# Third token mixer (HGRN2): at six of seven levels, scores only for one half of each block's queries, one bank per head, one copy out of it

## The reference, cut to what matters

```python
b = jnp.cumsum(gc, axis=2)
diff = b[:, :, :, None, :] - b[:, :, None, :, :]
pair_decay = jnp.where(causal[:, :, None], jnp.exp(jnp.minimum(diff, 0.0)), 0.0)
att = jnp.einsum('bhtd,bhsd,bhtsd->bhts', qc, kc, pair_decay)
o = jnp.einsum('bhtd,bhdv->bhtv', qc * jnp.exp(b), S) + jnp.einsum('bhts,bhsv->bhtv', att, vc)
```

## Time and profile before

| | |
|---|---|
| median of three runs | 2317.7 us |
| the profiled execution's own time | 2330.55 us |
| its span | 2328.8 us |
| TensorE matmul busy | 1913.3 us (82%) |
| TensorE weight load busy | 1544.2 us (66%) |
| VectorE busy | 1189.9 us (51%) |
| ScalarE busy | 662.1 us (28%) |
| mean granted TensorE clock | 0.864 of full speed |

### The profile page before, as it was taken

One profiled execution on the slowest core, in us unless ns is written; L12 is line 12 of the kernel. 1 busy time (PEld: TensorE's weight loads), 2 busy tenths in 40 slices (PEclk: granted clock), 3 DMA queues, 4 the chain that ended last, 5 costly groups with the idle time before them and its releaser, 6 DMA issues. The chain is left out here.

```text
span 2328.8 us, 28837 instructions
## 1 busy us (share of the span) xinstructions
PE 1913.3 (82%) x11780; PEld 1544.2 (66%) x11780; DVE 1189.9 (51%) x1853; ACT 662.1 (28%) x982; POOL 139.8 (6%) x160
## 2 busy tenths in 40 slices
PE   7997994787497986699999969899464989858996
PEld 5666773454396964588877756687343979648985
DVE  2473465652763523644442355446747745255655
ACT  3334324211220202422222253332412211034333
POOL 0000110000030300000000000000000303000000
PEclk9998996785698968799999979899686989678999
DMA  8201111670000003322222011122220000026441
GB/s 342 80 19 63 55 55 38 238 258 11 0 1 1 1 1 127 127 91 97 102 91 90 19 66 64 54 73 64 81 84 1 1 1 1 1 93 232 164 164 71
DMA packets 40884, 181.82 MB, mean 78 GB/s; under 512 B 4528, under 2 KB 5040, under 8 KB 32944
## 3 DMA queue, kind: packets, MB, share of 16 engines
q1 hardware_dynamic: 40752, 179.97, 21.8%
HBM read 178.91 MB, written 1.05 MB: 77 GB/s over the span
## 5 line engine op out<-in xcount | busy, mean ns | idle before, releaser
L211 PE MATMUL ps<-hr_in,wr_in 128*128 128x512 f32 (+1 forms) x544 | 224.8, 413 | 31.5 <-DVE wr_in L204 29.0
L211 PE MATMUL ps<-hr,wr 128*128 128x512 f32 (+1 forms) x704 | 240.4, 341 | 3.2 <-DVE wr L204 1.5
L212 PE MATMUL ps<-hr,wr 128*128 128x512 f32 (+1 forms) x704 | 237.5, 337 | 0.0
L213 PE MATMUL ps<-hr,wr 128*128 128x512 f32 (+1 forms) x704 | 237.3, 337 | 0.0
L212 PE MATMUL ps<-hr_in,wr_in 128*128 128x512 f32 (+1 forms) x544 | 211.9, 389 | 0.0
L213 PE MATMUL ps<-hr_in,wr_in 128*128 128x512 f32 (+1 forms) x544 | 211.5, 389 | 0.0
L204 DVE TENSOR_TENSOR wr<-pr,wr 128x2048 fp32r<-128x2048 f32 (+1 forms) x58 | 115.8, 1997 | 135.7 <-ACT wr L200 135.7
L211 PEld LDWEIGHTS ps<-hr_in,wr_in 128*128 128x128 f32 x544 | 109.7, 202 | 84.0 <-issue 33.7
L211 PEld LDWEIGHTS ps<-hr,wr 128*128 128x128 f32 x704 | 134.5, 191 | 21.9 <-DVE wr L204 6.7
L2108 ACT COPY pr<-ps 128x512 f32<-128x512 f32 x96 | 56.3, 587 | 324.1 <-PE ps L1747 324.1
L212 PEld LDWEIGHTS ps<-hr,wr 128*128 128x128 f32 x704 | 134.6, 191 | 13.7
(11 more groups left out here) (383 smaller groups left out, 3512.0 us busy)
## 6 DMA issues: line engine op xcount, KB each, us to landing
mix<-in_w_in SPq DMA_DIRECT2D x68, 512.0 KB, 3.6
pr<-in_w_up SPq DMA_DIRECT2D x28, 1024.0 KB, 4.9
ring<-in_ada_w SPq DMA_DIRECT2D x44, 512.0 KB, 4.6
mix<-in_w_up SPq DMA_DIRECT2D x16, 1024.0 KB, 5.0
hx<-in_ada_w SPq DMA_DIRECT2D x28, 512.0 KB, 6.4
pr<-in_w_down SPq DMA_DIRECT2D x14, 1024.0 KB, 4.9
pr<-in_ada_w SPq DMA_DIRECT2D x8, 1024.0 KB, 15.7
pr<-in_w_out SPq DMA_DIRECT2D x16, 512.0 KB, 7.1
```

What stands on the lines that cost most here:

```text
L211: nc.tensor.matmul(out, sh, mh, start=first, stop=False)
L212: nc.tensor.matmul(out, sh, ml, start=False, stop=False)
L213: return nc.tensor.matmul(out, sl, mh, start=False, stop=last)
```

## The change

For l = 0 nothing changes. For l > 0:

- `parts_of(n)` gives one part, with all tiles, in place of a part for each pair of tiles. `products(n)` counts the parts of the steps before n, and replaces `n * len(pairs)` in every wait.
- A matmul has as its moving operand only the half of each block's queries that counts, 64 columns in pieces of B/2 out of every B. The stationary operand stays as it was, the 128 keys. So the scores of one q for all tiles lie in one bank: eight times 64 columns in layer 0, four times 64 in layer 1. The number of matmuls is as before.
- `collect` copies each bank once, reading contiguous columns. In layer 0 this is two copies a step of 512 elements a partition, in place of four of 256. In layer 1 it is two of 256 as before.
- A step with l > 0 uses two banks and one raise of `s_mm`, so the six banks hold three steps in place of one and a half (layer 0).

```diff
-    pairs = tuple((j, j + 1) for j in js[::2])
+    whole = tuple((j, j + 1) for j in js[::2])
+    def parts_of(n):
+        return whole if steps[n][1] == 0 else (js,)
+    def products(n):
+        return sum(len(parts_of(k)) for k in range(n))
...
-            return ps[(2 * (n * len(pairs) + m) + q) % SCORES]
+            return ps[(2 * (products(n) + m) + q) % SCORES]
...
-                for m, jj in enumerate(pairs):
-                    used = 2 * (n * len(pairs) + m + 1)
+                for m, jj in enumerate(parts_of(n)):
+                    used = 2 * (products(n) + m + 1)
                     if used > SCORES:
                         pe.wait_ge(S("at"), used - SCORES)
-                    for b in range(4):
+                    for b in range(2 * len(jj)):
                         t0 = (b % 2) * T + jj[b // 2] * P
                         for q in range(2):
-                            mm = nc.tensor.matmul(score_bank(n, m, q)[:, b * P:(b + 1) * P], keys[d][q * HD:(q + 1) * HD, t0:t0 + P],
-                                                  queries[d][q * HD:(q + 1) * HD, t0:t0 + P], start=True, stop=True)
+                            key, query = (t[q * HD:(q + 1) * HD, t0:t0 + P] for t in (keys[d], queries[d]))
+                            out, n_out = score_bank(n, m, q), P
+                            if l:
+                                query, n_out = query.rearrange("p (b t) -> p b t", t=2 << l), HD
+                                query = query[:, :, 1 << l:] if d == 0 else query[:, :, :1 << l]
+                            mm = nc.tensor.matmul(out[:, b * n_out:(b + 1) * n_out], key, query, start=True, stop=True)
...
-                    o = d * 2048 + jj[0] * 512
+                    o, count = d * 2048 + jj[0] * 512, 2 * len(jj)
                     for q in range(2):
-                        dst = at[:, o:o + 1024].rearrange("p (b q t) -> p b q t", b=4, q=2)[:, :, q, :]
-                        src = score_bank(n, m, q)[:, :].rearrange("p (b t) -> p b t", b=4)
+                        dst = at[:, o:o + 256 * count].rearrange("p (b q t) -> p b q t", b=count, q=2)[:, :, q, :]
+                        src = score_bank(n, m, q)
...
-                            dst, src = (v.rearrange("p b (k t) -> p b k t", t=B)[:, :, :, part] for v in (dst, src))
+                            dst = dst.rearrange("p b (k t) -> p b k t", t=B)[:, :, :, part]
+                            src = src[:, 0:HD * count].rearrange("p (b k t) -> p b k t", b=count, t=B // 2)
```

More of the change, by code:

```diff
@@ L1399, in _ @@
                     job(p)
-            pe.wait_ge(S("at"), 2 * len(pairs) * len(steps))
+            pe.wait_ge(S("at"), 2 * products(len(steps)))
             for hd in range(HEADS):
@@ L1496, in factors @@
                 if n >= 2:
-                    dve.wait_ge(S("s_mm"), len(pairs) * (n - 1))
+                    dve.wait_ge(S("s_mm"), products(n - 1))
                 nc.vector.tensor_tensor(later(queries[d], d, l), later(expo[d], d, l), later(tiles(pr, T_HQ, 2), d, l), ALU.mult)
@@ L1504, in collect @@
                 B = 2 << l
-                for m, jj in enumerate(pairs):
-                    dve.wait_ge(S("s_mm"), len(pairs) * n + m + 1)
-                    o = d * 2048 + jj[0] * 512
+                for m, jj in enumerate(parts_of(n)):
+                    dve.wait_ge(S("s_mm"), products(n) + m + 1)
+                    o, count = d * 2048 + jj[0] * 512, 2 * len(jj)
                     for q in range(2):
-                        dst = at[:, o:o + 1024].rearrange("p (b q t) -> p b q t", b=4, q=2)[:, :, q, :]
-                        src = score_bank(n, m, q)[:, :].rearrange("p (b t) -> p b t", b=4)
+                        dst = at[:, o:o + 256 * count].rearrange("p (b q t) -> p b q t", b=count, q=2)[:, :, q, :]
+                        src = score_bank(n, m, q)
                         if l == 0:
-                            mask = c(C_BASE + d * P).bitcast(I32).rearrange("p (b t) -> p b t", b=1).to_broadcast([P, 4, P])
+                            src = src[:, :].rearrange("p (b t) -> p b t", b=count)
+                            mask = c(C_BASE + d * P).bitcast(I32).rearrange("p (b t) -> p b t", b=1).to_broadcast([P, count, P])
                         else:
                             part = slice(B // 2, B) if d == 0 else slice(0, B // 2)
-                            dst, src = (v.rearrange("p b (k t) -> p b k t", t=B)[:, :, :, part] for v in (dst, src))
+                            dst = dst.rearrange("p b (k t) -> p b k t", t=B)[:, :, :, part]
+                            src = src[:, 0:HD * count].rearrange("p (b k t) -> p b k t", b=count, t=B // 2)
                             mask = halves(c(C_LEVEL + (d * LEVELS + l) * P).bitcast(I32), B, d == 0).to_broadcast(list(dst.shape))
@@ L1603, in _ @@
                 if n >= 2:
-                    act.wait_ge(S("s_mm"), len(pairs) * (n - 1))
+                    act.wait_ge(S("s_mm"), products(n - 1))
                 nc.scalar.activation(sooner(keys[d], d, l), sooner(expo[d], d, l), ACT.Exp, scale=-1.0).then_inc(S("k_exp"), 1)
```

## The result

The changed kernel takes 2350.3 us (median of 4 runs, 2342.3 to 2355.8) beside 2319.2 us for the kernel before (4 runs, 2317.5 to 2323.4). The ratio is 1.013, 95% interval 1.009 to 1.016: slower by some 31 us. The forecast was slower by 5.8 us, 2323.5, range to 2333; the sign was right and the size was not.

The account below looks back on a forecast made before the run. Layer 0's score loop was taken as bound by TensorE and the loads its jobs pace. Terms: -1 (copies, tails, waits), +5.8 and +1 (clock in layers 0 and 1), +5.8 on the median 2317.7: 2323.5 us, range 2307 to 2333.

Parts of the forecast that it names:

- The cadence: Score matmuls: time per instruction goes with the stationary operand's 128 columns, so halving moving columns gains 0.
- the tail: End of a step's last score matmul: at most 0.08 us saved in each of 24 steps, 2 us together.
- E: Rival: the score matmuls halve in time after all, -11 us, 2307 us; chance 0.08.
- The copies: Layer 0 score copies on VectorE: 0.16 us less in 10 steps, 0.6 in 2 at l = 1, 2.8 us together.
- The bank wait: TensorE's second scores of two steps wait 2.2 us together for banks; both waits go.
- what is late next: Second gate product, waiting 0.59 us for VectorE, starts sooner only by the copies; so 0.5 of 2.2 us gained.
- The clock: Score loops: rises come later on thinner work; layer 0 +5.8 us for two of five rises, layer 1 +1.
- the give-back: Layer 0's loop: shorter DMA waits return 1.4 us of each coefficient step's 4.3 us at the lower clock, leaving 2.9.
- rival B: Late rises plus layer 1's output at the lower clock, 17.1 us, +7.7, giving 2331 us; chance 0.18.
- C: Rival: change hidden, clock follows other work, only copies and banks give 0 to 2 us, 2316.5 us; chance 0.22.
- D: Rival: a shifted clock entry speeds layer 0's output by 13.6 us, up to 3 lost in the loop, 2307; chance 0.15.
- The median: Profiled execution was 12.9 us longer than the runs' median; the forecast difference was put on the median, 2317.7 + 5.8.

Follow-up runs that it names:

- e10: Changed kernel plus five extra matmuls of 512 moving columns ahead of the output in both layers, scores still at 64 moving columns: 2334.3 us.
- e3: Kernel before plus five extra matmuls of 512 moving columns ahead of the output in both layers: 2310.5 us, ratio 0.998 to the kernel before.
- e12: Kernel before plus two extra matmuls ahead of layer 0's output only: 2309.5 us, ratio 0.994 to the kernel before.
- e1: Changed kernel with 128 moving columns again in seven matmuls of eight (layer 1: three of four): 2319.3 us, ratio 1.001 to the kernel before.
- e5: Changed kernel plus pairs of extra 512-column matmuls in layer 0's loop, ahead of jobs that follow a coefficient spread: 2338.1 us.
- e7: Changed kernel with 64 moving columns in layer 0 alone, layer 1 mostly at 128 again: 2337.2 us, ratio 1.008 to the kernel before.
- e8: Changed kernel with every second matmul of a q at 128 moving columns, the others at 64: 2328.4 us, ratio 1.006 to the kernel before.

## Why the prediction was wrong

**The cadence: right.** Half the moving columns left it where it was; the 0.06 us a step that went is the tail, as bounded. That it goes with the stationary operand's 128 columns is not shown: no run changed them, and the earlier trace rows have 62 ns with 64 rows and 118 with 128 rows at the same 128 columns. E fell with this.

**The copies: right in sum for l = 2 and above, wrong at l = 1.** I took 0.6 us less in each of 2 steps; nothing went. The copy is slow there by how it writes `at` or reads the mask, not by how it reads the bank. Of it only the last copy was seen on the path: TensorE's wait for it ahead of layer 0's output went from 1.6 to 1.5 us.

**The bank wait: right.** No wait of the scores for copies is left in layer 0's loop. The waits of the changed kernel there (waiter, releaser: total us, times, longest):

```profile
PE ps L382 <- DMA hx<-in_ada_w: 6.9, 10, 1.3
...
PE ps L382 <- DMA ring<-in_ada_w: 5.5, 6, 1.4
...
PE ps L1358 <- DVE gate L1455: 3.2, 2, 2.4
```

The gate products now wait 3.2 us in place of 2.2. The prediction had named them as what is late next, but had them start somewhat sooner; so the banks' 2.2 us came back by about half.

**The clock: the term that failed, right in kind and mis-sized threefold in layer 0's loop.** I put +5.8 us on it: two rises late by one coefficient step, 4.3 us each less 1.4 that DMA waits give back. The loop measured +17.8 in this execution. Both factors were too small. First the count. These are the stretches at the upper level in the loop, before and then after (length, busy time and instructions of TensorE, granted clock, DMA), cut a little inside their ends:

```profile
426.60:439.80 13.20, 9.54 (x112) 1.00 0.61 211
447.00:460.20 13.20, 11.18 (x140) 1.00 0.49 174
471.00:480.90 9.90, 7.92 (x100) 1.00 0.72 245
485.00:497.80 12.80, 9.21 (x108) 1.00 0.68 230
502.00:511.40 9.40, 7.36 (x104) 1.00 0.72 249
522.20:532.00 9.80, 7.32 (x100) 1.00 0.32 118
```

```profile
425.40:431.60 6.20, 5.21 (x70) 1.00 0.81 285
439.20:442.20 3.00, 1.62 (x16) 1.00 0.87 243
459.40:465.80 6.40, 5.30 (x80) 1.00 0.84 292
480.00:486.20 6.20, 4.69 (x68) 1.00 0.88 297
500.40:506.60 6.20, 4.63 (x68) 1.00 0.92 296
528.00:530.80 2.80, 1.93 (x24) 1.00 0.97 303
545.00:547.60 2.60, 2.48 (x36) 1.00 0.03 6
```

There are seven rises where there were six, but the stretches last 3 to 6 us in place of 9 to 13. Together they are 68 us before and 33 after. I had asked only whether the clock rises later on thin work. The first rise is not late at all, 11 us behind the loop's start in both; what goes first is the length of the stretch behind it, 13 us before and 6 after. The clock also falls earlier, and for that the prediction had no term. (It also read four rises in layer 1's loop, all over scores; there are five, and the one at 1703.0 us comes over a job.) The mean says the same: the upper share is 0.28 of 134.8 us, where it was 0.62 of 117. Second the give-back. TensorE's busy time grew by 20.4 us (92.3 to 112.7), but its waits for loads shrank only from 13.6 to 6.9 + 5.5 = 12.4 us. A slot is filled again when TensorE has used it, so a slower TensorE also asks for its loads later. So 1.2 us came back from loads, where I had 2.8 for just two steps; all idle time together shrank by 2.6, which leaves the 17.8. By my own prices the 20.4 us are nearly five coefficient steps at 4.3 us.

**Layer 1's output: the rival B was what happened**, at its price: 16.8 us for the 17.1 worked out. It had 0.18. Its condition held: no rise comes in the last 15 us ahead of the output, with TensorE busy for 13.4 of them:

```profile
1732.40:1747.40 15.00, 13.37 (x98) 9.67 (x98) 7.61 (x19) 3.92 (x8) 0.00 (x0) 0.50 0.06 22
```

e10, with the same thin loop, has this output at 1.00 and 9.4 us once extras lift the clock ahead of it. The loop took +2.8 where I had +1. With the measured terms in place of mine the sum is 2317.7 + 17.8 + 2.8 + 7.4 = 2346. C fell with the clock's mean, and D did not happen: layer 0's output stayed at 30.0 us.

**The median.** I laid the profile's difference on the median of the runs. In the profiles the changed kernel is 22.8 us longer, in the medians 31. e3's and e12's profiles show 13 us less in layer 0's output where the medians show 7 to 11. Both would fit if the timed runs of the kernel before had that output at the upper clock now and then. But single profiles also differ where nothing was edited: from the end of layer 0's output to the start of layer 1's loop they take 1114 us in the kernel before and in e1, 1110 in the changed kernel, 1108 in e10 and 1104 in e3. Each kernel has one profile and the timed runs show no stretches, so this stays open.

## What to carry to other kernels

Before thinning a matmul, see which operand sets its cadence: with the same stationary operand, half the moving columns cost the same time here. Then ask what the clock does when the same instructions stream half the columns; in a loop full of waits, and the output behind it, that cost 31 us of 2319. When a long, dependent run of matmuls sits at 0.50 while TensorE is never idle, look at the idle gap ahead of it: two extra matmuls there took 13 us off the stretch in the profile and 11 off the median.

## What was not expected of the hardware

- TensorE with no idle time for 30.0 us stayed at 0.50, and the same 112 instructions stayed at 1.00 for 16.9 us behind two or five extras. Entering at 1.00 alone did not do it: in e5, e7 and e8 the clock fell 1.6 to 2.2 us into an output.
- More work raised the clock (0.64 to 0.87 in the loop) and brought the median from 2350.3 to 2338.1 us, with 18 matmuls of 512 moving columns added.
- The same 952 instructions of a thin loop took 132.1 us in one profile and 118.9 in another.
- `copy_predicated` into pieces of two columns takes 1.21 us for 512 elements and 0.60 for 256, against 0.65 and 0.36 in longer pieces, whether the bank is read at a stride or in one run.
